# Output projection of a hybrid decoder layer: eight full tiles against four pairs by seven half products

## What is computed

```python
merged = g_a * (y_a @ w_out_ssm) + g_b * (y_b @ w_out_att) + g_c * (y_c @ w_out_sc)
x = x + gate1 * (merged @ w_o)                      # the output projection, 1024 x 1024
h = rms_norm(x, norm2_w) * (1 + scale2) + shift2    # feeds the router
x = x + gate2 * hier_moe(h)                         # top-1 group, top-2 experts, 32 experts
```

## Time and profile before

| | us |
|---|---|
| median of 3 runs | 1487.93 (1487.29 to 1493.44) |
| profiled execution, its own time | 1488.65 |
| its span | 1486.9 |
| TensorE matmul busy | 1356.9 (91%) |
| VectorE busy | 663.2 (45%) |
| ScalarE / POOL busy | 257.7 / 140.7 |
| mean granted TensorE clock | 0.950 |

### The profile page before, as it was taken

One profiled execution on the slowest core, in us unless ns is written; L12 is line 12 of the kernel. 1 busy time (PEld: TensorE's weight loads), 2 busy tenths in 40 slices (PEclk: granted clock), 3 DMA queues, 4 the chain that ended last, 5 costly groups with the idle time before them and its releaser, 6 DMA issues. The chain is left out here.

```text
span 1486.9 us, 19377 instructions
## 1 busy us (share of the span) xinstructions
PE 1356.9 (91%) x7089; PEld 979.0 (66%) x7089; DVE 663.2 (45%) x1371; ACT 257.7 (17%) x554; POOL 140.7 (9%) x270
## 2 busy tenths in 40 slices
PE   4999999999999999899989988999989888787884
PEld 2787677888778788576767766888878632222333
DVE  1635677555667766110115567685631411111125
ACT  2201111222222521110122222410001300000001
POOL 0223000000000000122210002000001111111111
PEclk9999999999999999899999997999999988999895
DMA  8563223323323323455561011422244499999944
GB/s 339 170 136 107 96 63 120 115 76 108 114 68 99 109 62 123 153 178 189 182 240 45 30 43 72 166 64 84 74 176 180 174 364 426 425 424 423 400 152 181
DMA packets 62208, 250.87 MB, mean 169 GB/s; under 512 B 10058, under 2 KB 20714, under 8 KB 53002
## 3 DMA queue, kind: packets, MB, share of 16 engines
q1 hardware_dynamic: 42130, 185.31, 34.1%
q10 hardware_dynamic: 10264, 44.97, 8.4%
q0 software_dynamic: 9728, 19.42, 3.9%
HBM read 234.47 MB, written 22.91 MB: 173 GB/s over the span
## 5 line engine op out<-in xcount | busy, mean ns | idle before, releaser
L350 PE MATMUL psum<-arena 128*128 128x272 f32 x2048 | 485.5, 396 | 5.0 <-PEq L1460 4.0
L350 PEld LDWEIGHTS psum<-arena 128*128 128x128 f32 x2048 | 389.5, 191 | 96.7 <-issue 11.1
L362 PE MATMUL psum<-arena 128*128 128x272 f32 x840 | 197.3, 394 | 0.0
L362 PEld LDWEIGHTS psum<-arena 128*128 128x128 f32 x840 | 157.6, 189 | 39.8 <-issue 6.7
L1203 PE MATMUL psum<-arena 128*128 128x272 f32 x512 | 126.1, 405 | 0.0
L2442 PE MATMUL psum<-arena 128*64 128x512 f32 x512 | 115.1, 601 | 2.7 <-DVE arena L2541 2.7
L1203 PEld LDWEIGHTS psum<-arena 128*128 128x128 f32 x512 | 98.5, 195 | 26.7 <-DVE arena L1334 4.1
L2442 PEld LDWEIGHTS psum<-arena 128*64 128x64 f32 x512 | 35.8, 136 | 70.9 <-issue 70.9
L1334 DVE TENSOR_TENSOR arena<-arena,psum 128x272 f32<-128x272 f32 x16 | 7.0, 438 | 141.2 <-ACT arena L1286 141.2
L2463 PE MATMUL psum<-arena 128*64 128x512 f32 x256 | 68.8, 686 | 1.2 <-DVE arena L2530 1.2
L1522 PE MATMUL psum<-arena 128*128 128x272 f32 x256 | 63.6, 402 | 2.9 <-PEq L206 2.9
(11 more groups left out here) (374 smaller groups left out, 1420.0 us busy)
## 6 DMA issues: line engine op xcount, KB each, us to landing
arena<-in_weights SPq DMA_DIRECT2D x153, 512.0 KB, 4.4
arena<-in_w_gu SPq DMA_DIRECT2D x32, 2048.0 KB, 17.3
arena<-in_w_down ACTq DMA_DIRECT2D x28, 1024.0 KB, 16.1
arena<-in_weights ACTq DMA_DIRECT2D x16, 512.0 KB, 4.2
arena<-in_x SPq DMA_DIRECT2D x2, 2176.0 KB, 10.9
arena<-in_pages_k POOLq DMA_DIRECT2D x32, 128.0 KB, 3.1
arena<-in_pages_k SPq DMA_DIRECT2D x32, 128.0 KB, 2.4
arena<-in_pages_v SPq DMA_DIRECT2D x32, 128.0 KB, 3.1
```

The source lines that it names most:

```text
L350: mm = pe.matmul(out[:, h, :], lhsT=w_of(n, c), rhs=act[:, c, h * HALF:(h + 1) * HALF], start=(c == 0), stop=(c == DC - 1))
L362: mm = pe.matmul(out, lhsT=w[:, c * P:c * P + P], rhs=x[:, c, :], start=(c == 0), stop=(c == 3))
```

## The change

The output projection takes two tiles at a time through the seven half products, and the two blocks become one, so that no barrier stands between the merge and the output projection. In detail:

- TensorE: 4 pairs (v = 0 to 3) of 7 products, 4 matmuls each, in place of 8 tiles of 16. Product j of the 28 goes to bank (j + 4) % 8. Product 0 waits for two merged pairs (`s_mgw` 2: chunks 0 to 3), product 1 for all four, products 2, 3 and 4 for the second, third and fourth activation sum. After pair 0, TensorE waits for its own product 6, then lets SP load the down weights. The gate-up permission is given at product 1.
- The two tiles of a pair are taken in swapped order (`SWAPPED`), so that the even chunk is complete at k = 5 and the odd one at k = 6.
- VectorE: the weight sums of pair 0 are made within w = 7, the first activation sum after w = 3 (as soon as chunks 0 to 3 are merged), the other three after the last merge. Then for each pair 8 block steps, the 4 weight sums of the next pair, and two residuals, which now read the finished tile from SBUF (`tm10`) in place of PSUM.
- The sums lie in `wsum[:, 0]`, in space of the third gate-up place, and in ring places whose tiles are done; `t_m[0]` and the partial tiles lie behind the first gate-up place.
- ScalarE's warm-up of Sqrt writes to `small`; POOL's small table and its memset come behind the last residual.

```diff
@@ seven_blocks, next_sum
-                        if w + 1 < N_SEVEN:
-                            weight_sum(dve, n + 2, wsum[:, (w + 1) % 2], k, sum_link)
+                        weight_sum(dve, n + 2, wsum[:, (w + 1) % 2], k, sum_link, SWAPPED if w + 1 == N_SEVEN else (0, 1))
@@ after an odd w, on VectorE
-                    link(dve.tensor_tensor(merged[:, w - 1:w + 1, :], merged[:, w - 1:w + 1, :], tmw, ALU.add))
+                    dve.tensor_tensor(merged[:, w - 1:w + 1, :], merged[:, w - 1:w + 1, :], tmw,
+                                      ALU.add).then_inc(s_mgw, 1)
+                    dve.wait_ge(s_mgw, w // 2 + 1)
+                    if w == 3:
+                        act_link(dve.tensor_tensor(t_m[0], block_of(merged, 0, 1), block_of(merged, 0, 0), ALU.subtract))
@@ TensorE
-        with nc.Block() as block:
+                for v in range(4):
+                    n = T_O + 2 * v
+                    for k, (wv, x) in enumerate(seven_operands(n, sums_o[v], merged, t_m, SWAPPED)):
+                        j = 7 * v + k
+                        if k == 0:
+                            tile_ready(pe, n + 1)
+                            pe.wait_ge(s_mgw, 2)
+                        if j == 1:
+                            pe.wait_ge(s_mgw, 4)
+                            pe.sem_inc(s_gu, 2)
+                        if k == 2:
+                            pe.wait_ge(s_wsum, 4 * (N_SEVEN + v) + 2)
+                            pe.wait_ge(s_asum, 10)
...
+                        pe.wait_ge(s_took, 53 + j if j < 4 else max(56, 49 + j))
+                        mm = half_product(pe, psum[:, (j + 4) % 8, 0:HALF], wv, x)
+                        if k < 6:
+                            mm.then_inc(s_prod, 1)
+                    mm.then_inc(w_used, 2)
+                    if v == 0:
+                        pe.wait_ge(w_used, T_O + 2)
+                        pe.sem_inc(s_dn, 2)
-                for u in range(8):
-                    tile_ready(pe, T_O + u)
-                    if u >= 4:
-                        pe.wait_ge(s_res, u - 3)
-                    project(pe, T_O + u, pair[u % 4], merged).then_inc(w_used, 1)
@@ VectorE
+                for out, a, b in ((t_m[1], block_of(merged, 1, 1), t_m[0]),
+                                  (t_m[2], block_of(merged, 1, 1), block_of(merged, 0, 1)),
+                                  (t_m[3], block_of(merged, 1, 0), t_m[1])):
+                    act_link(dve.tensor_tensor(out, a, b, ALU.subtract))
+                for v in range(4):
...
+                        block_step(dve, k, psum[:, (7 * v + k + 4) % 8, 0:HALF], (part10[:, 0, :], part10[:, 1, :]),
+                                   blocks_of(tm10), took)
+                        for i in {2: (0, 1), 3: (2,), 5: (3,)}.get(k, ()):
+                            if v < 3:
+                                weight_sum(dve, n + 2, sums_o[v + 1], i, sum_link, SWAPPED)
+                        if k >= 5:
+                            if v == 0 and k == 5:
+                                dve.wait_ge(s_x10, 16)
+                            residual(2 * v + k - 5, tm10[:, 6 - k, :])
@@ POOL
+                pool.wait_ge(s_res, DC)
+                pool.tensor_tensor(dshift, mods[:, 24:32, 1:NSEQ], mods[:, 24:32, 0:1].to_broadcast([P, DC, NB]),
+                                   ALU.subtract).then_inc(p_link11, 1)
+                pool.memset(xg, 0.0).then_inc(s_rows, 1)
```

More of the change, by code:

```diff
@@ L369, in act_sums, with tile_halves, weight_sum @@
                 link(dve.tensor_tensor(out, a, b, ALU.subtract))
[L371 to L377, removed]
+        def tile_halves(n, order=(0, 1)):
+            return [ring[:, (n + i) % RING, 512 * k:512 * k + 512] for i in order for k in range(2)]
+        def weight_sum(dve, n, sums, k, link, order=(0, 1)):
+            a11, a12, a21, a22 = tile_halves(n, order)
             if k == 0:
@@ L2042, in build @@
[L2042 to L2057, removed]
@@ L2081, in build @@
[L2081 to L2104, removed]
@@ new lines, in build @@
+            s_h2w = [sem(f"h2_written{i}") for i in range(4)]
+            acc11 = A.at(a_e + 4 * NT, NT)
+            sq11 = A.at(a_e + 5 * NT, 4, NT)
+            assert a_e == a_free and a_free + 10 * NT <= a_xb and a_w + 8 * D == a_sums
+            a_r11 = a_w + 8 * D
+            std11 = A.at(a_r11, P)
+            std_new = A.at(a_r11 + P, NEW)
+            lgT = A.at(a_r11 + 160, 256)
+            lgT_new = A.at(a_r11 + 416, NEW, parts=36)
+            rcol = A.at(a_r11 + 448, 5)
+            dshift = A.at(a_r11 + 456, DC, NB)
@@ new lines, in build @@
+            full = [A.at(a_r + 720 + 160 * k, NR, NE) for k in range(2)]
+            both = A.at(a_r + 1040, NR, NE)
+            tmp32 = A.at(a_r + 1200, 2, NR, NE)
+            rank = A.at(a_r + 1520, 2 * NR)
+            p2 = A.at(a_r + 1530, NR)
+            mx = A.at(a_r + 1567, 16)
+            tabf = A.at(a_r + 1583, NP)
+            pick = A.at(a_r + 1600, 2, 2 * NR, NE)
+            slot_of = A.at(a_r + 2240, 2 * NR, CAP)
+            xn11 = A.at(a_r + 2240, DC, NEW)
+            pre = A.at(a_r + 2240 + 2 * NR * CAP, NR, NE)
@@ new lines, in build @@
+            wtab = A.at(a_r + 2400 + 2 * NR * CAP, NP)
+            wcol = A.at(a_param + PARAM_AT["conv_prev"][0], 2, NR)
+            a_keep = a_param + PARAM_AT["conv_prev"][0] + 16
+            rounds_i = A.at(a_keep + 20, 1).bitcast(I32)
+            rows11 = A.at(a_xb + DC * NT - 2 * D, 4, D)
+            assert T_O % RING + 3 < RING and T_END - T_O == RING
+            sums_o = [wsum[:, 0], A.at(a_xb + DC * NT, 4, 512)] + [
+                A.at(a_ring + (T_O + 2 * v) % RING * 1024, 4, 512) for v in range(2)]
@@ L2139, in _, with residual @@
                 link = link_of(dve, v_link10)
+                sum_link, act_link, took = link_of(dve, s_wsum), link_of(dve, s_asum), link_of(dve, s_took)
                 tmp = A.at(a_r + 2420 + 2 * NR * CAP, NEW)
[L2141 to L2149 removed]
+                def residual(m, src):
+                    gate, dst, new = mods[:, 16 + m, :], xT[:, m, 0:SEQ], xT[:, m, SEQ:NT]
+                    dve.scalar_tensor_tensor(dst, src[:, 0:SEQ], gate[:, 0:1], dst, ALU.mult, ALU.add)
+                    link(dve.tensor_tensor(by_seq(tmp), by_seq(src[:, SEQ:NT]), per_seq(gate), ALU.mult))
```

149 lines of the change are left out of this document (84 added, 65 removed).

## The result

| | before | changed |
|---|---|---|
| median, runs of this comparison | 1489.51 us (1487.29 to 1493.44, 6 runs) | 1480.63 us (1478.28 to 1483.35, 6 runs) |
| ratio | | 0.9943, 95% interval 0.9921 to 0.9966 |
| median over all comparisons of the study | 1490.1 us (84 runs) | 1480.0 us (28 runs) |
| mean over the same | 1490.1 us | 1480.5 us |
| span of the profiled execution | 1486.9 us | 1480.4 us |

The forecast was 1475.3, its range 1472.5 to 1479.0. The kernel became faster, by 8.9 us in this comparison and by 10.1 over all runs, where 12.6 were forecast. The median lies 1.6 us above the range. The 84 runs are those of the kernel before that stood beside the other versions.

The account below looks back on a forecast made before the run. The interval from the merge's last product to the router's first matmul was taken to hold up the experts' weight stream. Gains 7.4 (products), 2.6 (gap), 3.2 (clock), less 0.3 and 0.25: 1487.93 - 12.6 = 1475.3 us, range 1472.5 to 1479.0.

Parts of the forecast that it names:

- Seven products: Output projection: seven products for eight, 12.87 in place of 14.72 us per pair of tiles, four pairs save 7.4 us.
- The barrier: Between merge and output projection: TensorE idle 1.45 us behind product 0 in place of 4.03, a gain of 2.6 us.
- Activation sums: Three sums by 1.29 us behind the last merge are ready before products 2, 3 and 4 want them: no wait.
- The clock: Start of the output projection: clock stays full through the 1.45 us gap, so the 3.16 us lost before come back.
- the rival: Clock falls in the 1.45 us gap behind product 0: price 1.7 to 3.2 us, total 1477.0 to 1478.5, chance 0.12.
- VectorE's load: Output projection pairs: VectorE needs 8.7 of 12.87 us for steps, weight sums and residuals, hidden behind TensorE.
- The drain: After pair 0 TensorE waits for its own product 6 and its pipe drains once: 0.3 us, bounded by 0.46.
- The hand-over to the router: Router's matmuls wait for residual 6, 0.25 us more; the last residual and its square stay covered by 0.8 us.
- The rule weighed: VectorE and POOL slow each other adding from SBUF: at worst 11.4 of 12.87 us per pair, cover overdrawn by 0.5.
- serial start: Output projection's start: TensorE waits for merge and three sums, 5.3 us gap plus clock loss; 1482.4 us, chance 0.04.
- VectorE the bound: Four pairs: operations with two SBUF inputs stretched threefold beside POOL, 19.1 us per pair; 1505 us, chance 0.02.
- it doesn't reach the end: Experts' weight stream starts no earlier, because the slot table or a transfer sets it: 1487.9 us, chance 0.03.

Follow-up runs that it names:

- all three small edits: Second early product, down-weight permission two products later, and POOL's table and memset behind the scaling, on the changed kernel: 1475.61 and 1478.44 us, ratios 0.9921 and 0.9923.

## Why the prediction was wrong in its number and right in most of its mechanism

1. **Seven products** (7.4 us): right. Products by 1.84 us, TensorE busy all the time but for three gaps. The run with all three small edits gives 51.75 us for 28 products and the hand-over.
2. **The barrier** (2.6): right to 0.1 by the rows, a gap of 1.51 in place of 1.45. In the interval this gap cost 1.76, by the run that fills it; a stop's own 0.25 was nowhere in the sum.
3. **Activation sums**: right, no wait at products 2, 3 and 4.
4. **The clock** (3.16): right but for 0.2. The half clock over the matmuls from 1104.56 to 1110.48 is worth 2.96 us; the 0.2 left is about what the gap of 1.51 us cost beyond its row, and that isn't given back. Clock 1.00 through the stage in all four profiles of the changed kernel, and back to 0.50 with a gap of 3.3 or 3.9 us. But the row it rested on was weaker than it looked: the gap of 1.86 us left the clock at 1.00 in the first profile, and had a fall to 0.50 right behind it in the second of the same kernel and in 10 of all 18. The 0.12 given to the rival rested on one draw of this fall. Of gaps of 1.51 us in this place none of six had a fall.
5. **VectorE's load**: right. By the rows' own times 8.6 us a pair, 9.7 where one residual meets POOL's addition (1.33 us for 0.19), and it idles before most steps.
6. **The drain** (0.3): cost 0.55, by the run that takes it away. The bound of 0.46 was too low. The 0.25 too little here, 0.3 at the gap and 0.04 at the hand-over are the stage's 0.6: 12.0 for 12.6.
7. **Transfers**: right, the down weights didn't matter.
8. **The hand-over to the router**: the wait of 0.29 was forecast at 0.25. What failed is the sentence "POOL's memset has moved behind it and is due only after the row scales". I asked when the memset was due, and not who works beside it: table and memset hold up VectorE's scaling of chunk 7, 2.30 us for 0.49. And the last residual was done 2.73 us behind the router's first matmul, where 1.75 was forecast, since L2180 was held up by POOL's addition. The rule weighed foresaw that collision; the cover was enough for it alone, and for both it wasn't. The last logits start 5.25 us behind the router's first matmul in place of 4.54, and the router stretch is 25.34 us on average in the six profiles before and 25.89 in the four after. The Trainium skill, "SBUF — State Buffer", section "SBUF: two separate sides", names VectorE operations in a two-port mode beside those with two SBUF inputs as the ones that GpSimd can shut out. The rows agree in that L2204 has one SBUF tensor and waited; no run shows in which mode it ran.
9. **The range** is the step that put the number outside: "runs of one kernel vary by about a microsecond". The runs of before went from 1482.64 to 1496.77 over the study. The 1487.93 from which I subtracted was the median of three; it lies 1.6 below the median of before in the comparison and 2.2 below that of 84. The profiles show the places: the clock's falls behind short gaps in the stages up to the merge, which come or not from run to run.

The forecast of 1475.3 missed the 1480.63 by 5.3 us: 1.6 by the base, 0.6 in the stage and 0.55 in the router. The last 2.6 are that this comparison gave 8.9 us where stage and router give 12.0 - 0.55 = 11.5. Over all runs the shortfall is 1.4 us by the medians and 1.9 by the means, the latter more than the runs' spread explains. Its cause is open. The merge's pairs take the same 103.11 us in all profiles; behind the router stretch the profiles of the two kernels differ by 0.3 us on average, and the means of the merge's end would give it, but they don't differ by more than their spread. The rivals "serial start" and "VectorE the bound" are out by the timeline; "it doesn't reach the end" is out by the totals.

## What to carry to other kernels

A barrier in front of a full matmul stage costs its gap and then the clock, here 4.03 and 3.16 us; one piece of work that depends on nothing late, put where the gap was, won back 2.5 us of the gap and all of the clock's loss. When work is moved into another engine's idle time, look at who works beside it at that moment and whether that one has slack, not only at its own deadline. And before a forecast of 1%, look at how far runs of the same kernel lie apart: a stage's interval in the profile repeated to 0.1 us here, where totals wandered by 14. An interval alone doesn't prove the total, though: here some 1 to 2 us of it didn't arrive.

## What the runs showed of the hardware

- TensorE's clock (1.2 or 2.4 GHz granted) behind idle gaps in the same place of the program: 4.03 us of idle, half clock in six of six profiles of before; 3.89 and 3.30 us, half clock, in one each; 1.51 us, full clock in six of six. Elsewhere, 2.32 us: half clock in 18 of 18; 1.86 us: in 10 of 18, with the same code.
- The end of the merge wandered over 1097 to 1106 us while the merge's own pairs took 103.11 us each time. Where it ended past 1105, 61.4 or 64.9 us at half clock lay ahead of it, elsewhere 51.2 to 58.0.
- A POOL addition of 0.29 us and a memset of 1.81, back to back, stretched a VectorE operation of 128x512 with one SBUF tensor, started in the same hundredth, from 0.49 to 2.30 us; it ended 0.27 us behind the memset.
- TensorE waiting for its own last matmul before a semaphore operation: 0.30 us idle in the row, 0.55 us in the interval. A gap of 1.51 us: 1.76 us in the interval.
